# First mLSTM head begun with its values, tile by tile of x, with the gates as eight more columns

## What is computed

```python
proj = rmsnorm(x) @ w_in                      # q, k: 4 x 128; v, o: 4 x 256; gates: 2 x 4
gates = 15 * tanh((gates + b_gates) / 15)
ig, fg = split(gates); lf = log_sigmoid(fg)
b = cumsum(lf); D = b_t - b_s + ic_s          # per chunk and head, causal
m_t = max(b + m, max_s D)
Sw = (q k^T) * exp(D - m_t)
h  = (Sw v + exp(b + m - m_t) * C q) / max(|den|, exp(-m_t))
```

## Time and profile before

| | us |
|---|---|
| median of 3 runs | 2027.62 (2027.56 to 2028.22) |
| the profiled execution | 2027.4 |
| its span | 2025.8 |
| TensorE busy | 1990.9 (98%) |
| VectorE / ScalarE / GpSimd busy | 1332.3 / 922.3 / 1212.4 |
| mean granted TensorE clock | 0.996 |

### The profile page before, as it was taken

How to read it: one execution, slowest core, us unless ns; L and a number is a source line. 1 busy time by engine, 2 the same in 40 slices (tenths; PEclk the granted TensorE clock), 3 DMA queues, 4 the chain that set the end, 5 groups by cost and what they waited for, 6 DMA issues and landing times.

```text
span 2025.8 us, 28802 instructions
## 1 busy us (share of the span) xinstructions
PE 1990.9 (98%) x9992; PEld 1660.0 (82%) x9992; DVE 1332.3 (66%) x1737; ACT 922.3 (46%) x1911; POOL 1212.4 (60%) x1058
## 2 busy tenths in 40 slices
PE   7899999999999999999999999999999999999998
PEld 6888989788888888888888777788888888888886
DVE  7654552578777777554666576779766676645567
ACT  6444343365555555422236455546454454432233
POOL 5432520574889888756564312373979788746565
PEclk9999999999999999999999999999999999999999
DMA  6655645753777877795863222463677776697673
GB/s 157 196 184 177 204 154 219 271 170 122 229 255 235 263 244 238 251 360 212 266 211 65 52 94 63 158 206 112 211 247 236 235 233 226 205 341 284 217 264 130
DMA packets 295428, 415.00 MB, mean 205 GB/s; under 512 B 40040, under 2 KB 218232, under 8 KB 295296
## 3 DMA queue, kind: packets, MB, share of 16 engines
q1 hardware_dynamic: 260752, 307.87, 46.6%
q10 hardware_dynamic: 33120, 100.68, 13.8%
q0 software_dynamic: 1424, 4.77, 0.8%
HBM read 259.09 MB, written 154.17 MB: 204 GB/s over the span
## 4 chain that ended last, share of the span: by engine, by line
PE 89%; DVE 5%; issue 2%; ACT 2%; DMA 1%; POOL 0%; SPq 0%; ACTq 0%; DVEq 0%; POOLq 0%
PE ps L2286 22%; PE ps L2288 22%; PE ps L2287 22%; PE ps L2189 8%; PE ps L2191 4%; PE ps L2578 1%; PE ps L2409 1%; PE ps L2410 1%; PE ps L2406 1%; PE ps L2539 1%; PE ps L2341 1%; DVE forms L1807 1%; PE ps L2598 1%; DVE mats L1709 1%; PE ps L2460 1%
## 5 line engine op out<-in xcount | busy, mean ns | idle before, releaser
L2286 PE MATMUL ps<-forms,mats 128*128 128x512 f32 x2016 | 788.3, 391 | 6.9 <-ACT part L1358 2.3
L2288 PE MATMUL ps<-forms,mats 128*128 128x512 f32 x2016 | 784.9, 389 | 0.0
L2287 PE MATMUL ps<-forms,mats 128*128 128x512 f32 x2016 | 784.5, 389 | 0.0
L1065 POOL TENSOR_TENSOR mats<-sum_a,mats 128x256 fp32r<-128x256 f32 (+2 forms) x384 | 405.0, 1059 | 359.2 <-ACT mats L1297 358.3
L2286 PEld LDWEIGHTS ps<-forms,mats 128*128 128x128 f32 x2016 | 378.4, 188 | 92.3 <-issue 13.5
L2288 PEld LDWEIGHTS ps<-forms,mats 128*128 128x128 f32 x2016 | 378.4, 188 | 79.4
L2287 PEld LDWEIGHTS ps<-forms,mats 128*128 128x128 f32 x2016 | 378.5, 188 | 77.5
L1732 DVE TENSOR_TENSOR X<-ps,X 128x512 f32<-128x512 f32 x390 | 268.2, 690 | 191.4 <-PE ps L2288 189.6
L1297 ACT ACTIVATE mats<-sum_a 128x256 fp32r<-128x256 f32 (+2 forms) x392 | 201.3, 515 | 310.0 <-PE ps L2288 295.7
L1709 DVE TENSOR_TENSOR mats<-stream_raw,mats 128x256 fp32r<-128x256 f32 (+2 forms) x302 | 281.1, 933 | 19.6 <-ACT mats L1297 18.9
L1297 ACT ACTIVATE mats<-stream_raw 128x256 fp32r<-128x256 f32 (+2 forms) x302 | 156.4, 519 | 243.8 <-PE ps L2288 242.6
(11 more groups left out here) (233 smaller groups left out, 2645.3 us busy)
## 6 DMA issues: line engine op xcount, KB each, us to landing
forms<-scratch_forms ACTq DMA_DIRECT2D x182, 512.0 KB, 5.5
scratch_forms<-prep_forms SPq DMA_DIRECT2D x161, 512.0 KB, 3.5
stream_raw<-in_w_gate_up_dram SPq DMA_DIRECT2D x88, 512.0 KB, 5.5
scratch_forms<-head_forms SPq DMA_DIRECT2D x49, 512.0 KB, 2.6
scratch_hidden<-hidden SPq DMA_DIRECT2D x84, 256.0 KB, 5.3
prep_raw<-in_w_down_dram SPq DMA_DIRECT2D x38, 512.0 KB, 5.4
stream_raw<-scratch_hidden SPq DMA_DIRECT2D x32, 512.0 KB, 4.7
forms<-scratch_forms SPq DMA_DIRECT2D x28, 512.0 KB, 5.1
```

The source lines that it names most:

```text
L1065: pool.tensor_tensor(blocks(m[:, q, 1, :], it.width), stream_source(it, q), blocks(m[:, q, 0, :].bitcast(F32), it.width), ALU.subtract).th ...
L2286: mm(dst, ah, bh, start=OPENS[q] and k == 0, stop=False, skip_group_check=True)
L2287: mm(dst, ah, bl, start=False, stop=False, skip_group_check=True)
L2288: m = mm(dst, al, bh, start=False, stop=k == w - 1, skip_group_check=True)
```

## The change

The values of head 0 come first and take the gates with them.

- SP loads two tiles of x, then the 256 value columns of head 0 in three pieces of K (3, 3 and 2 tiles), then the rest of x. ScalarE's own queue issues the load of the 8 gate columns beside them and that of the norm's gains, ahead of its first square.
- The gain is folded into the split of that weight (ScalarE's scale, a VectorE scalar_tensor_tensor), 8 slices of 264 columns instead of a GpSimd product.
- TensorE makes value tile t (24 matmuls of 264 columns: 256 values and 8 gates) as soon as tile t of x is transposed; the transposes run one tile ahead. The 48 gate matmuls of 512 columns, and `v_tiles` of head 0, are gone. Query and key follow.
- bias, tanh, exp, ln and the products of the gates are done on 128x64 or 128x32 (tokens on partitions). 1/(1+exp) is a VectorE reciprocal where an exp of ln was. Then 8 transposes of `gate_windows` inside the query columns bring them to rows of 4x1024, which ScalarE copies; the scans and what follows stay as they were (neg_M now ahead of G). The transposes of G are inside the key columns.
- The forms of row 0, 7 of them, leave the value tiles and go into chunks 0 to 3, two at a time; those of row 1 into chunks 4 to 7. In the first head, three `write_lo` stand ahead of the first chunk's work on VectorE.
- Units 0 to 2 are the three pieces; query, key and output gate of head 0 are units 3 to 6. `load_unit(1, 1)` is moved ahead of SP's wait for the gates.

```diff
+        VG = DV + 2 * NH_A
+        vraw = at("v_gates_raw", [P, KT, VG], o_R)
+        vh = at("v_gates_hi", [P, KT, VG], o_ring, F32R)
+        vl = at("v_gates_lo", [P, KT, VG], o_T + TILE, F32R)
...
-            for t in range(3):
+            for t in range(2):
                 load_x(t)
...
+            v0 = 2 * NH_A * DQK
+            for j, (k0, k1) in enumerate(VK):
+                sp.dma_start(vraw[:, k0:k1, 0:DV], win[:, k0:k1, v0:v0 + DV]).then_inc(v_loaded[j], 16)
+            for t in range(2, TT):
                 load_x(t)
...
+            load_head(0, 0, range(2, 5))
+            sp.dma_start(bgate[:].rearrange("p a h -> p (a h)"), a_b_gates[0, :].partition_broadcast(P)
                          ).then_inc(bgate_loaded, 16)
-            load_head(0, 0, range(2, 6))
+            load_head(0, 0, (5,))
...
             load_unit(1, 0)
-            sp.wait_ge(gate_dve, 12)
-            sp.wait_ge(gate_act, 7)
+            load_unit(1, 1)
+            sp.wait_ge(gate_dve, 13)
+            sp.wait_ge(gate_act, 9)
             load_head_row(0)
-            load_unit(1, 1)
             load_unit(1, 2)
...
+            g0 = 2 * NH_A * DQK + 2 * D
+            act.dma_start(vraw[:, :, DV:VG], win[:, :, g0:g0 + 2 * NH_A]).then_inc(gate_w_loaded, 16)
+            act.dma_start(gcol[:, 0, :], a_norm[0, :].rearrange("(k p) -> p k", p=P), allow_slow_non_contiguous=True
+                          ).then_inc(a_gain_loaded, 16)
             K = uses.stage(NORM)
...
+            Kv = [uses.stage(BANK_4567) for _ in range(2)]
+            def square_of_tile(t):
+                act.wait_ge(x_loaded[t], 16)
+                square(0, t)
+            def v_hi(j):
+                if j == 0:
+                    act.wait_ge(a_gain_loaded, 16)
+                    act.wait_ge(gate_w_loaded, 16)
+                act.wait_ge(v_loaded[j], 16)
+                for k in range(*VK[j]):
+                    hi = act.activation(vh[:, k, :], vraw[:, k, :], ACT.Copy, scale=gcol[:, 0, k:k + 1])
+                hi.then_inc(hi_ready, 1)
+            def v_out(t):
+                b = 4 + t % 4
+                act.wait_ge(bank_full[b], Kv[t // 4][b] + 1)
+                g = act.activation(gp[:, :, t, :], ps[:, b, DV:VG].rearrange("p (a h) -> p a h", a=2), ACT.Copy)
+                if t == TT - 1:
+                    g.then_inc(gate_act, 1)
+                if t == 0:
+                    act.wait_ge(xs_ready, 5)
+                act.activation(v1[:, t, 0:DV], ps[:, b, 0:DV], ACT.Copy).then_inc(bank_free[b], 1)
+            square_of_tile(0)
+            square_of_tile(1)
+            xt_hi(K, 0)
+            v_hi(0)
+            xt_hi(K, 1)
+            v_hi(1)
+            v_hi(2)
+            square_of_tile(2)
+            for t in range(3, TT):
+                square_of_tile(t)
+                xt_hi(K, t - 1)
+                if t >= 5:
+                    v_out(t - 5)
+            xt_hi(K, TT - 1)
+            for t in range(3, TT):
+                if t < 6:
+                    write_hi(Unit(t))
+                v_out(t)
...
+            act.wait_ge(gate_dve, 1)
+            act.activation(gp[:], gp[:], ACT.Tanh, scale=1.0 / GATE_CAP).then_inc(gate_act, 1)
+            act.wait_ge(gate_act, 2)
+            act.activation(ge[:], gp[:, 1], ACT.Exp, scale=-GATE_CAP).then_inc(gate_act, 1)
+            act.activation(table_col[:], keep_le[:, 0:1], ACT.Ln)
+            act.wait_ge(gate_dve, 3)
+            act.activation(gl[:], gu[:], ACT.Ln).then_inc(gate_act, 1)
+            act.wait_ge(gate_act, 4)
+            act.activation(table_col[:], neghalf[:, 0:1], ACT.Exp)
             K = uses.stage(BANK_45)
-            act.wait_ge(gate_dve, 1)
             for half in range(2):
-                c = slice(half * 512, (half + 1) * 512)
                 b = 4 + half
                 act.wait_ge(bank_full[b], K[b] + 1)
...
+                f_row = act.activation(lf[:, half * 512:(half + 1) * 512], ps[32:32 + NH_A, b, :], ACT.Copy)
+            f_row.then_inc(gate_act, 1)
+            for half in range(2):
+                b = 4 + half
+                act.activation(ig[:, half * 512:(half + 1) * 512], ps[0:NH_A, b, :], ACT.Copy).then_inc(bank_free[b], 1)
+            write_hi(Unit(6))
...
+            query_out(uses.stage(BANK_01))
+            act.wait_ge(gate_dve, 9)
+            act.activation(G[32:32 + NH_A, :], mrow[:], ACT.Exp, scale=-1.0).then_inc(gate_act, 1)
+            act.wait_ge(gate_dve, 13)
+            act.activation(G[64:64 + NH_A, :], brow[:], ACT.Exp).then_inc(gate_act, 1)
+            act.activation(einter[:], diff[:], ACT.Exp).then_inc(gate_act, 1)
+            act.activation(mprev[:, 2, :], mprev[:, 1, :], ACT.Exp).then_inc(gate_act, 1)
...
-                        if first and t < NQ:
-                            head_row_hi(0, t)
...
-                    if first and c:
-                        head_row_hi(1, c - 1)
+                    if first:
+                        for q in range(2 * (c % 4), min(NQ, 2 * (c % 4) + 2)):
+                            head_row_hi(c // 4, q)
...
+            def v_lo(j):
+                dve.wait_ge(hi_ready, j + 1)
+                for k in range(*VK[j]):
+                    lo = dve.scalar_tensor_tensor(vl[:, k, :], vraw[:, k, :], gcol[:, 0, k:k + 1],
+                                                  vh[:, k, :].bitcast(F32), ALU.mult, ALU.subtract)
...
+            xt_lo(0, K, 0)
+            v_lo(0)
+            xt_lo(0, K, 1)
+            v_lo(1)
+            v_lo(2)
...
+            dve.wait_ge(bgate_loaded, 16)
+            dve.wait_ge(gate_act, 1)
+            dve.tensor_tensor(gp[:], gp[:], bgate[:].unsqueeze(2).to_broadcast([P, 2, TT, NH_A]), ALU.add
                               ).then_inc(gate_dve, 1)
-            write_lo(Unit(U_HEADS + 2))
+            windows = Gw[:, 0:2 * TT * NH_A].rearrange("p (a t h) -> p a t h", a=2, t=TT)
+            dve.wait_ge(gate_act, 2)
+            dve.tensor_scalar(windows[:, 0], gp[:, 0], GATE_CAP, None, ALU.mult).then_inc(gate_dve, 1)
+            dve.wait_ge(gate_act, 3)
+            dve.tensor_scalar(gu[:], ge[:], 1.0, None, ALU.add).then_inc(gate_dve, 1)
+            dve.wait_ge(gate_dve, 3)
+            dve.scalar_tensor_tensor(gc[:], gu[:], -1.0, ge[:], ALU.add, ALU.subtract).then_inc(gate_dve, 1)
+            dve.reciprocal(gr[:], gu[:]).then_inc(gate_dve, 1)
+            dve.wait_ge(gate_dve, 5)
+            dve.tensor_tensor(gc[:], gc[:], gr[:], ALU.mult).then_inc(gate_dve, 1)
+            dve.wait_ge(gate_dve, 6)
+            dve.wait_ge(gate_act, 4)
+            dve.tensor_tensor(windows[:, 1], gc[:], gl[:], ALU.subtract).then_inc(gate_dve, 1)
...
-                    for q in range(3, NQ):
-                        head_row_lo(0, q)
+                    write_lo(un[2] + LEAD)
+                    write_lo(un[3] + LEAD)
                     dve.wait_ge(decay_loaded, 16)
...
-                    if first and c:
-                        head_row_lo(1, c - 1)
+                    if first:
+                        for q in range(2 * (c % 4), min(NQ, 2 * (c % 4) + 2)):
+                            head_row_lo(c // 4, q)
...
+            def v_gate_tile(t):
+                b, xv = 4 + t % 4, slice(t * P, (t + 1) * P)
+                pe.wait_ge(bank_free[b], Kv[t // 4][b])
+                dst = ps[:, b, 0:VG]
+                for k in range(KT):
+                    if k % 4 == 0:
+                        xb = 2 * (t % 2) + k // 4
+                        pe.wait_ge(bank_free[xb], Kn[xb] + t // 2 + 1)
+                    for j, (k0, _) in enumerate(VK):
+                        if t == 0 and k == k0:
+                            pe.wait_ge(lo_ready, j + 1)
+                    m = mm(dst, xh[:, k, xv], vh[:, k, :], start=k == 0, stop=False)
+                    if t == 0 and k == 0:
+                        begin(m)
+                    mm(dst, xh[:, k, xv], vl[:, k, :], start=False, stop=False)
+                    m = mm(dst, xl[:, k, xv], vh[:, k, :], start=False, stop=k == KT - 1)
+                m.then_inc(bank_full[b], 1)
+            def gate_windows():
+                pe.wait_ge(gate_dve, 7)
+                for t in range(TT):
+                    b = 4 + t // 4
+                    if t % 4 == 0:
+                        pe.wait_ge(bank_free[b], Kw[b])
+                    m = nc.tensor.transpose(ps[:, b, (t % 4) * P:(t % 4 + 1) * P], Gw[:, NH_A * t:NH_A * t + P], ident[:])
+                    if t % 4 == 3:
+                        m.then_inc(bank_full[b], 1)
+            def gate_rows():
+                pe.wait_ge(gate_act, 7)
+                for j in range(2):
+                    pe.wait_ge(bank_free[6 + j], Kg[6 + j])
+                    for c in range(4):
+                        t = 4 * j + c
+                        m = nc.tensor.transpose(ps[:, 6 + j, c * P:(c + 1) * P], G[:, t * P:(t + 1) * P], ident[:])
+                    m.then_inc(bank_full[6 + j], 1)
+            for t in range(2):
```

(17 more changed lines are left out.)

274 lines of the change are left out of this document (102 added, 172 removed).

## The result

Twenty runs of each kernel on one chip: before 2027.43 us (median), after 2030.53, a ratio of 1.0015 with the interval 1.0008 to 1.0022. The change makes the kernel 3.1 us slower. Forecast was 3.7 us faster; the range ended at 2029.5.

What follows compares the result with a forecast made beforehand. TensorE, 89% of the chain that ended last, was taken as the bound. Chunk 0 starting 5.4 us earlier, less 1.7 us lost in the chunks, gave -3.7: from 2027.6 to 2023.9 us, range 2016 to 2029.5.

Steps and rivals of the forecast that it cites:

- X: The end of head 0's last value tile on TensorE, forecast at 46.2 us with 0.8 charged for the clock.
- The clock in the value tiles: Gaps between the first value tiles lower TensorE's granted clock; charged with 0.8 us, a third of 2.5.
- rival B: TensorE's clock stays at half through the value tiles; three slow tiles give +4.8 us, 2032.4; chance 0.12.
- Gate functions and windows hidden: Ahead of the window transposes, gate functions of 3.5 us are covered by five K-steps of 6.8 us on TensorE.
- rival D: Query columns wait for the windows; 3 us of margin against it; folded into rival C, no chance of its own.
- From the first scan's start to the end of the last exp: Head 0's scans to last exp stay 11.65 us, only one swap inside, so they end at X + 20.4.
- Legs of e_inter: Store and load back of e_inter ahead of chunk 0: 6.9 and 3.9 us, landing at X + 31.2.
- rival A: e_inter's store takes 2.6 us, its load 3.9; chunk 0 at 80.5, total -9.0 us, 2018.6; chance 0.16.
- Half clock behind the long wait: TensorE idles 9 us ahead of the output-gate columns and its clock falls; charged with 1.4 us before chunk 0.
- together 1.7 us back: Head 0's chunks lose 0.5 us ahead of chunk 4 and 1.2 through row 1's late load and VectorE in chunk 5.
- rival C: Row 1's load, stores and VectorE's subtractions are slower, so the chunks lose 3 us more: 2026.9; chance 0.12.
- Everything later is moved by the difference, one for one: Everything behind the chunks of head 0 shifts by the whole net gain, -3.7 us.

Runs made afterwards that it cites:

- e1_same: The changed kernel run again with no edit: 2029.76 us, ratio 1.0015 to the kernel before (2026.87 us on its chip).

## Why the prediction was wrong

- **The start**: right. First transposes at 7.64 (7.5 forecast), value matmuls from 12.90 (13), tile 2's matmuls from 24.8 (23.5), X at 45.9 (46.2, or 45.4 without the clock, which stayed full in this profile). The small loads on ScalarE's queue cost 0.1 us: its first square began at 4.73 instead of 4.62.
- **The clock in the value tiles**, charged with 0.8 us, and rival B: in the profile of after it was 0, in six of ten profiles 2.0 to 2.9 us. The mechanism is right, but it was never the 8.5 us of rival B. That this is why most executions lie above the one in profile is likely and not shown, since only one execution of each kernel has a profile.
- **Gate functions and windows hidden** (rival D false): right, no wait of TensorE at the windows; ahead of the gate rows, forecast to be hidden by 2 us, it waited 0.80, for the reason that follows.
- **"From the first scan's start to the end of the last exp ... nothing in it is changed"**: wrong by 3.2 us. The scans were moved beside GpSimd's gains of units whose loads had moved too. I followed each queue's order, but not which work of two engines now meets.
- **Legs of e_inter**: store leg 5.7 us (6.9 forecast), load leg 3.9 (3.9); rival A's 2.6 did not come. inter_row 1.5 us instead of 2.9. Together 2.6 too much.
- **Half clock behind the long wait**, charged with 1.4: measured 2.5, half of it ahead of chunk 0's start and half behind. So counted as the prediction counts, chunk 0 came at 85.50 + 1.2 = 86.7, against 85.8. That it came so near is luck: 3.2 and 1.1 too little, 2.6 too much. (Two of its figures do not follow from its terms: rival A's landing at X + 27.5 has legs that make X + 26.9, and halfway from the forecast to rival B is 2028.2, not the 2029.5 at which the range ends. Neither decides anything.)
- **The chunks "together 1.7 us back"**: this is the term of the sum that was mis-sized. Measured 5.6 us (34.0 us from chunk 0 to 7 against 28.4), of which 1.2 are the clock behind the first wait, charged to the start; so 4.3 stand against the 1.7. They are 2.6 us of waits for `C_state`, 1.6 of half clock behind them, which no term had, and 0.1 more. The place (row 1's late load, VectorE late in chunk 5) was named, and rival C, with 1.7 + 3 us, had nearly the size.
- **"Everything later is moved by the difference, one for one"**: the step that failed outright. Head 0 ended when it did before, and the kernel was 3.1 us slower. From the wait near 1689 us on, the changed kernel takes 338.5 us (338.7 in e1_same) against 336.8 before, and all profiles with a block of instructions beside the store are slow there, those without are not; padding alone takes 2.4 us from that stretch and 2.8 off the median. Between head 0 and that wait the two profiles differ by 1.2 us the other way (1554.9 us after, 1556.2 before, 1556.2 in e1_same), which hides most of it in the pair. No row of before shows a wait to come; what could have shown it is the queue of instructions, and I did not read it.

So the 3.1 us are, by the runs: nothing gained in head 0 (5.7 earned, 5.6 spent), some 2 us for the place of the blocks (1.7 and 1.8 against the kernel before, 2.4 against padding, in profiles), and up to 2.9 in executions whose clock falls in the value tiles. Settled is the first and the second; the share of the third in the median is not, since each kernel has one profile.

## To carry to other kernels

Work moved to make one wait shorter meets other work: list for each moved stretch what the neighbouring engine does at its new time, and which queue item hangs on the last buffer freed there. An early start is only worth what the next bound lets through: price that bound first, here by leaving out one load. And when a change of a few instructions moves a long kernel by a tenth of a per cent far from the edit, compare waits stage by stage and pad the program before believing in the edit's own effect.

## What the runs showed of the hardware

- TensorE's instruction blocks come over the same DMA engines as data: with one packet of 16 KB beside a 512 KB store that was waited for, that wait was 3.5 to 4.0 us (nine profiles) instead of 2.1 to 2.6 (eight), and some 256 instructions more brought the packet back to the same place.
- VectorE's operation with two inputs in SBUF beside GpSimd's: 1.22 us became 2.2 to 4.3, once 6.95, always ending 1.1 us behind GpSimd's last instruction beside it; two of GpSimd's own took 6.2 us instead of 3.8 beside the scans. Each reads as if it waited for the other's whole instruction. The Trainium skill, "GPSIMD Engine Reference", 1. Specifications, says that the SBUF interfaces are shared with VectorE, with contention for such instructions; the rows agree and give it a size.
- The granted clock of a stretch is not fixed by the program: the same instructions from 12 to 37 us had 1.00 in four executions, 0.86 in five and 0.93 in one.
- A product of `ident` in f32 with four columns is two matmuls and took 0.43 us ahead of the first transposes and 0.24 us just behind them; the same with the split operands took 0.12 us (36 in 4.4 us), and 0.18 when 92 of them ran, most at half clock.
